# Expert rows fetched by indirect DMA from DRAM, slot numbers made on TensorE, and three more weight units loaded ahead

## The reference, cut to what matters

```python
def expert_choice_ffn(h, w_router, w_gate, w_up, w_down):
    cap = CAPACITY_FACTOR * S // N_EXPERTS                       # 64
    aff = jax.nn.softmax((h @ w_router).astype(jnp.float32), axis=-1)
    gates, idx = lax.top_k(aff.transpose(0, 2, 1), cap)          # each expert picks 64 tokens
    xe = h[bidx, idx]                                            # [expert, 64, 1024]
    hg = jnp.einsum('becd,edf->becf', xe, w_gate)
    hu = jnp.einsum('becd,edf->becf', xe, w_up)
    y = jnp.einsum('becf,efd->becd', jax.nn.silu(hg) * hu, w_down)
    y = y * gates[..., None].astype(y.dtype)
    return jnp.zeros_like(h).at[bidx, idx].add(y)                # scatter back
```

## Time and profile before

| | us |
|---|---|
| median of three runs | 2327.1 |
| the profiled execution, its own time | 2332.71 |
| its span, first to last instruction | 2330.9 |
| `experts`, first gather to the end | 1841.9 to 2330.9 |

### The profile page before, as it was taken

How to read it: one execution, slowest core, us unless ns; L and a number is a source line. 1 busy time by engine, 2 the same in 40 slices (tenths; PEclk the granted TensorE clock), 3 DMA queues, 4 the chain that set the end, 5 groups by cost and what they waited for, 6 DMA issues and landing times. The chain is left out here.

```text
span 2330.9 us, 31729 instructions
## 1 busy us (share of the span) xinstructions
PE 2087.4 (90%) x12841; PEld 1035.2 (44%) x12841; DVE 953.8 (41%) x1775; ACT 440.9 (19%) x877; POOL 238.9 (10%) x191
## 2 busy tenths in 40 slices
PE   6989898898998998989798977887789699999997
PEld 3453445643463343564343533455434444444442
DVE  1049668541026778752333542394321511111112
ACT  1011352121002144121312331321110200000000
POOL 0030410000020130000004530500000000000000
PEclk9999999999998999999899988998899799999999
DMA  4125110212214401121102101120055399999997
GB/s 158 68 107 198 46 39 26 75 46 69 80 48 172 163 10 39 35 101 36 48 18 73 37 28 48 62 77 34 11 163 207 128 403 419 421 420 420 420 420 290
DMA packets 63470, 330.03 MB, mean 142 GB/s; under 512 B 7280, under 2 KB 9840, under 8 KB 34928
## 3 DMA queue, kind: packets, MB, share of 16 engines
q1 hardware_dynamic: 63344, 328.27, 36.9%
HBM read 321.16 MB, written 6.29 MB: 140 GB/s over the span
## 5 line engine op out<-in xcount | busy, mean ns | idle before, releaser
L424 PE MATMUL ps<-store,side_ring 128*128 128x512 f32 x824 | 406.9, 623 | 15.8 <-DMA side_ring<-in_w_attn 7.1
L424 PEld LDWEIGHTS ps<-store,side_ring 128*128 128x128 f32 x824 | 146.0, 194 | 190.2 <-issue 168.3
L2565 PE MATMUL ps<-expert_ring,xe 128*64 128x512 f32 x1024 | 223.3, 593 | 4.0 <-DMA expert_ring<-in_w_expert 2.3
L337 PE MATMUL ps<-store,side_ring 128*128 128x512 f32 x384 | 169.9, 606 | 1.9 <-DVE store L303 1.9
L424 PE MATMUL ps<-store 128*128 128x512 f32 x256 | 122.1, 634 | 24.9 <-DMA store<-in_w_merge 24.4
L2565 PEld LDWEIGHTS ps<-expert_ring,xe 128*64 128x64 f32 x1024 | 73.0, 137 | 150.9 <-issue 148.7
L337 PEld LDWEIGHTS ps<-store,side_ring 128*128 128x128 f32 x384 | 74.5, 195 | 96.1 <-issue 93.5
L2593 PE MATMUL ps<-expert_ring,store 128*64 128x512 f32 x512 | 111.6, 594 | 1.4 <-DVE store L2650 1.4
L1645 PE MATMUL ps<-store,raw 128*128 128x512 f32 x256 | 110.7, 593 | 1.9 <-DVE store L303 1.9
L2622 ACT ACTIVATE store<-ps 128x1024 f32<-128x1024 f32 x16 | 16.4, 1025 | 417.8 <-PE ps L2565 417.8
L424 PEld LDWEIGHTS ps<-store 128*128 128x128 f32 x256 | 51.6, 204 | 93.1 <-issue 66.6
(11 more groups left out here) (430 smaller groups left out, 3051.4 us busy)
## 6 DMA issues: line engine op xcount, KB each, us to landing
expert_ring<-in_w_expert SPq DMA_DIRECT2D x192, 1024.0 KB, 17.1
mixed<-in_w_ada SPq DMA_DIRECT2D x24, 1024.0 KB, 4.8
side_ring<-in_w_attn SPq DMA_DIRECT2D x32, 512.0 KB, 3.9
side_ring<-in_w_rwkv SPq DMA_DIRECT2D x20, 512.0 KB, 4.4
raw<-in_ple_gate SPq DMA_DIRECT2D x16, 512.0 KB, 3.8
store<-in_w_merge SPq DMA_DIRECT2D x16, 512.0 KB, 4.1
side_ring<-in_w_conv SPq DMA_DIRECT2D x12, 512.0 KB, 3.3
gates_before<-gated SPq DMA_DIRECT2D x16, 256.0 KB, 2.0
```

The lines of the kernel that those rows point to most:

```text
L337: last = nc.tensor.matmul(ps[:, u, :], ring[:, u, k, :], src[:, k, :], start=(k == 0), stop=(k == kt - 1))
L424: ins = self.nc.tensor.matmul(self.ps[:, self.banks[j % banks], :], self.ring[:, j % self.slots, k, :], self.src[:, k, :], start=(k == 0), ...
L2565: last = nc.tensor.matmul(ps[w, 2 * ep + half, :], xe[:, ep, k, :], ring[:, unit % SLOTS, k2, S * half:S * half + S], start=(k == 0), stop ...
```

## The change

- **Rows.** SP writes `tokens` to DRAM as `token_rows` (four DMAs of 512 KB) once `h_copied` is complete. For pairs 1 to 7 POOL (GpSimd) fetches the 128 rows of a pair with one indirect DMA into a half of `rows` (the first two tiles of `tokens`). PE's gather becomes `turn_rows`: four transposes of the fetched rows after each eight transposes. The first pair's gather stays as it was.
- **Numbers.** `number` multiplies `chosen` of each later pair with a column of token numbers: 7 x 4 matmuls with one moving column, on PE between the first expert's products of pair 0 and `turn_back`. DVE casts the seven columns to integers.
- **Three units used once.** Units 0 to 2 of pair 0 go into places of their own, `once` (two in `back`, one new tile), issued when x is complete. The ring's first 12 units are then units 3 to 14, and SP's loop goes by turns of the ring.
- The loop over pairs has two pairs in its body, so that each unit's ring place is a constant. `route` takes its scratch from `chosen` instead of `back`.

The core of the diff:

```diff
@@ first_experts
-                sp.dma_start(ring[:, i], w_expert[0, i]).then_inc(landed[i], 16)
+                sp.dma_start(ring[:, i], w_expert[ONCE + i]).then_inc(landed[i], 16)
+            sp.wait_ge(added[0], added[1] + KT)
+            for i in range(ONCE):
+                sp.dma_start(once[i], w_expert[i]).then_inc(once_landed[i], 16)
@@ experts, sync
+                sp.wait_ge(h_copied, KT)
+                for t in range(TT):
+                    sp.dma_start(rows_out[t * P:(t + 1) * P, :], tokens[:, t, :]).then_inc(s["rows_out"], 16)
+                turns, rest = divmod(PAIRS * UNITS - ONCE, SLOTS)
+                with sp.Fori(1, turns) as turn:
+                    for i in range(SLOTS):
+                        sp.wait_ge(used[i], turn)
+                        sp.dma_start(ring[:, i], w_expert[turn * SLOTS + (ONCE + i)]).then_inc(landed[i], 16)
...
@@ experts, tensor
+                def number():
+                    for i in range(1, PAIRS):
+                        for t in range(TT):
+                            last = nc.tensor.matmul(ps[:, 3, i:i + 1], chosen[:, t, 2 * i:2 * i + 2, :].rearrange("p e c -> p (e c)"),
+                                                    M.c("token_number")[:, t:t + 1], start=(t == 0), stop=(t == TT - 1))
+                    last.then_inc(s["numbered"], 1)
+                def turn_rows(tiles, buf):
+                    for k in tiles:
+                        last = nc.tensor.transpose(ps[:, k // 4, (k % 4) * P:(k % 4 + 1) * P], rows[:, buf, k * P:(k + 1) * P],
+                                                   M.c("ident"))
+                        if k % 4 == 3:
+                            last.then_inc(s["gathered"], 1)
...
                             if first:
+                                number()
                                 turn_back()
...
                         if not final:
-                            gather(range(4 * ep, 4 * ep + 4), lambda t: chosen[:, t, bass.ds(r * 2 + 2, 2), :].rearrange("p e c -> p (e c)"))
+                            if ep == 0:
+                                pe.wait_ge(s["rows_landed"], r + 1)
+                            turn_rows(range(4 * ep, 4 * ep + 4), (1 + half_body) % 2)
@@ experts, gpsimd
+                pool.wait_ge(s["numbers_ready"], 1)
+                pool.wait_ge(s["rows_out"], 16 * TT)
+                pool.wait_ge(s["gathered"], 2)
+                for i in range(1, PAIRS):
+                    if i >= 3:
+                        pool.wait_ge(s["gathered"], 2 * (i - 1))
+                    nc.gpsimd.indirect_dma_start(rows[:, (i - 1) % 2, :], None, rows_out,
+                                                 bass.IndirectOffsetOnAxis(ap=numbers[:, i:i + 1], axis=0)).then_inc(row[i - 1], 16)
+                    pool.wait_ge(row[i - 1], 16)
+                    pool.sem_inc(s["rows_landed"], 1)
@@ experts, vector
+                dve.wait_ge(s["numbered"], 1)
+                nc.vector.tensor_copy(numbers[:, 1:PAIRS], ps[:, 3, 1:PAIRS]).then_inc(s["numbers_ready"], 1)
```

More of the change, by code:

```diff
@@ L2460, with slot_of, turn_of, first_experts @@
 PAIRS, UNITS, SLOTS = 8, 24, 12
-TURNS = UNITS // SLOTS
-def first_experts(nc, ring, w_expert, landed, busy, merge_taken, merge_done):
+BODY, ONCE = 2, 3
+TURNS = BODY * UNITS // SLOTS
+def slot_of(half, i):
+    return (UNITS * (1 + half) + i - ONCE) % SLOTS
+def turn_of(b, half, i):
+    return b * TURNS + (UNITS * (1 + half) + i - ONCE) // SLOTS
+def first_experts(nc, ring, once, w_expert, landed, once_landed, busy, merge_taken, merge_done, added):
     with phase(nc) as (block, s):
@@ L2485, in experts @@
         sb = lambda name, shape: buffer(nc, stack, name, shape)
-        xe = sb("xe", [P, 2, KT, 64])
+        xe, rows = sb("xe", [P, 2, KT, 64]), tokens[:, 0:2, :]
+        numbers = stack.enter_context(nc.sbuf_tensor(f"numbers_{nc.next_id()}", [P, PAIRS], U32))
+        w_expert = w_expert.rearrange("r u p k n -> (r u) p k n")
+        row = [stack.enter_context(nc.semaphore(f"row_landed_{i}")) for i in range(1, PAIRS)]
         flat = lambda first, tiles: room[:, first:first + tiles, :].rearrange("p k n -> p (k n)")
@@ L2499, in _ @@
             def _(sp):
[L2500 to L2507, removed]
+                sp.wait_ge(h_copied, KT)
[6 more added lines that the diff above has]
+                        sp.dma_start(ring[:, i], w_expert[turn * SLOTS + (ONCE + i)]).then_inc(landed[i], 16)
+                for i in range(rest):
+                    sp.wait_ge(used[i], turns)
+                    sp.dma_start(ring[:, i], w_expert[turns * SLOTS + ONCE + i]).then_inc(landed[i], 16)
+                sp.wait_ge(s["rows_landed"], PAIRS - 1)
                 for m in range(KT):
@@ L2602, in _ @@
                 pe.wait_ge(s["all_chosen"], TT)
[L2603 to L2606, removed]
+                pair(-1, 1, first=True)
+                with pe.Fori(0, PAIRS // BODY - 1) as b:
+                    for half_body in range(BODY):
+                        pair(b, half_body)
+                pair(PAIRS // BODY - 1, 0, final=True)
                 pe.wait_ge(s["out_ready"], PAIRS)
@@ L2641, in _, with pair @@
                 both = ps[:, 0:2, :].rearrange("p b (k e c) -> p e (b k) c", e=2, c=64)
-                def pair(r, first=False, final=False):
+                def pair(b, half_body, first=False, final=False):
+                    r = b * BODY + (1 + half_body)
                     if not first:
@@ L2674, in _ @@
                     nc.vector.tensor_copy(back[:, i, :], ps[:, 4 + i % 4, :]).then_inc(s["back_copied"], 1)
[L2675 to L2678, removed]
+                pair(-1, 1, first=True)
+                with dve.Fori(0, PAIRS // BODY - 1) as b:
+                    for half_body in range(BODY):
+                        pair(b, half_body)
+                pair(PAIRS // BODY - 1, 0, final=True)
                 for m in range(KT):
@@ L2724, in second_block @@
             ready = norm(nc, M, x, lambda k: gains[:, 1, k:k + 1], h, shift=lambda k: mcol(3, k), source=added)
[L2725 to L2728, removed]
+            h_copied, first_chosen = route(nc, M, a["w_router2"], h, ready, tokens, aff, chosen, slot,
+                                         chosen[:, :, :, :].rearrange("p t e c -> p t (e c)")[:, :, 0:S])
+            first_experts(nc, ring, once, a["w_expert2"].rearrange("r u p k n -> (r u) p k n"), landed, once_landed, busy, taken,
+                          multiplied, added)
+            experts(nc, M, a["w_expert2"], token_rows, tokens, chosen, aff, slot, extra[:, :], h, back, lambda j: mcol(5, j), x, out, ring, landed,
+                    once, once_landed, h_copied, first_chosen)
 def program(nc, a, out):
```

47 lines of the change are left out of this document (32 added, 15 removed).

## The result

The changed kernel takes 2339.43 us (median of 5 runs, 2337.67 to 2341.62), the kernel before 2327.1 us beside it (5 runs, 2325.43 to 2329.39): the ratio is 1.0054, with a 95% interval from 1.0038 to 1.007. It is slower, by 12.3 us between the medians; the forecast was 2336.4, 9.3 slower.

What follows compares the result with a forecast made beforehand. The weight stream on saturated DMA engines was taken as the bound, PE close behind. Terms -7.5 + 8.8 + 3.5 + 1.0 + 6.3 - 1.8 = +10.3 us, less 1.0 slack, gave +9.3: 2336.4 us, range 2332 to 2342.

Steps and rivals of the forecast that it cites:

- the hole: Empty weight stream behind pair 0's first expert, as number delays the second: +6.3 us left after two fetches fall into it.
- The bound: In the pairs, the saturated weight stream (DMA share 1.01, 420 GB/s) sets the end, slower than PE by 1.5 us a pair.
- Three units, -7.5: Three units of pair 0 move in idle time before the stream, which carries 177 units instead of 180: -7.5 us.
- first issue, +3.5: Start of the stream: the first ring place comes free one quarter later, at 1857.9, costing +3.5 us.
- Fetches, +8.8: Seven indirect fetches of 0.524 MB share the saturated engines with the weights at 1.25 us each: +8.8 us.
- the old stall: Stream's standstill of about 1.8 us from 1896 to 1900, during pair 0's transposes and gather, nearly closes: -1.8 us.
- Slack, -1.0: At the end, last bytes land about 1 us before use, so that much stream delay is absorbed: -1.0 us.
- Cheap numbers and free fetches: Rival: number takes only 1.7 us and fetches in the stream cost nothing; middle about 2329 us, no change, chance 0.22.
- TensorE the bound: Rival: PE limits the pairs, so seven shorter middles come back: -21 us, 2306 us, chance 0.08.
- A fetch on few engines: Rival: a fetch's rows go through one engine, 20 us each, holding the stream up to 140 us: up to 2467, chance 0.08.
- The clock in the pairs: Rival: PE's waits of some 1.5 us drop its clock to 1.2 GHz: +105 us, 2432 us, chance 0.04.

Runs made afterwards that it cites:

- e7: Changed kernel without numbers, row copies and fetches, rows gathered by products, keeping the three units used once: ratio 1.0006 to the kernel before.
- e3: Changed kernel with no units in places used once (ONCE = 0): ratio 1.0052 to the kernel before.
- e6: Changed kernel with each of the seven fetches issued a second time after the first landed: ratio 1.0092 to the kernel before.
- e2: Changed kernel without the seven indirect fetches and their wait: ratio 1.0033 to the kernel before.
- e5: Changed kernel with the number products streaming 64 repeated columns instead of one: ratio 1.005 to the kernel before.
- e1: Changed kernel without the 28 number matmuls; two small ones write other row numbers, same fetch traffic: ratio 1.0028 to the kernel before.
- e4: Changed kernel with number moved from before turn_back to behind the second expert's products: ratio 1.0072 to the kernel before.
- e8: Kernel before with turn_back moved to pair 1, units 4, 5, 12 used once, only pairs 1 and 2 fetched: 2323.1 us, ratio 0.9985.
- e9: e8 without its two fetches, their numbers and the row copy; all pairs gathered by products: ratio 1.0002 to the kernel before.
- e10: Kernel before with only turn_back moved from pair 0 to pair 1, ahead of its scatter: ratio 1.0008 to the kernel before.

## Why the prediction was right

The direction, the mechanism (the stream is the bound, PE's shorter middle buys nothing, PE waits for units) and the place of the hole came out as forecast. Size: the runs are 12.3 us slower and PE's last wait for a unit ends 12.4 us later, where 9.3 were forecast. The last landing came 13.7 us later relative to the first product, where 10.3 were forecast; 1.3 of that is a gap ahead of the last two units (3.8 us from one landing to the next instead of 2.5), behind PE's last wait; what made it is open. The terms that were off all erred the same way, so no luck is in the number: it was 3 us low, inside its range.

- *The bound.* Right: the earlier trace rows already held it, share 1.01 at 420 GB/s, and it is the same after. That PE had waited only 2.3 us was indeed no sign of spare transfer time.
- *Three units, -7.5, and first issue, +3.5.* The packets of e7's stream take 447.8 us instead of before's 454.6, -6.8, a little less than 7.5; the issue comes +3.46 later. Each term is about right, but the three units also leave the stream empty earlier at the next wait, so that together they are worth 0.1 us in the changed kernel (e3) and 0.3 alone (e7). The prediction held this in its hole, as five places given back instead of eight.
- *Fetches, +8.8.* Right: 9.2 for seven by e6's packets. To the last wait 5.5 us (e2), as two of the seven first fetches lie in the hole, and 8.8 us (e6). On this path POOL's transfers share the engines with SP's, as the Trainium skill (DMA: Bandwidth & Descriptors, section Issuing engines are not separate DMA queues) has it; e6's doubled fetches show it.
- *The hole, 6.3 + 1.0 - 1.8 = +5.5.* Near, with a part mis-sized. By the packets the engines stand idle 7.3 us longer (6.7 after; -0.6 before, in which the old stall of 1.8 lies, as such sums run over), 6.0 without the 1.3 of that gap. The old stall did close: the DMA share is 0.99 and 1.07 in the two stretches of 2 us from 1896 to 1900. `number` was taken at 6.2 us, from the records of the gather at 0.112 us each; it took 8.1, and `turn_back` 6.6 instead of 5.6, because the granted clock fell to half. The nearest row had 128 columns. e5, with 64, returns both to 6.3 and 5.6 us, the figures of the forecast; its last landing is 10.8 us later than before's, where the sum has 10.3.
- *Slack, -1.0.* Wrong: it should have been 0. It was read at the last unit, which landed at 2309.8 and was wanted at 2310.9. But PE's last wait stands 16 units earlier, and there PE waited 1.26 us before the change already, so a delay of the stream up to that unit reaches the end whole. The 13.1 us of the stage are these 12.4 and 1.5 of half clock in the last down products, less 0.9 by which the end behind the last scatter was shorter. (The estimate of 1 us from landing to use was too long as well: at this wait PE starts 0.14 us after the landing, in both kernels.)
- *The rivals.* Cheap numbers and free fetches: no (8.1 us; 1.32 us a fetch). TensorE the bound: no, PE waits 26.4 us. A fetch on few engines: no, 8.4 us median to landing against the 20 that it would have needed at least. The clock in the pairs: no, at 21 waits of up to 1.4 us PEclk is 1.00 from 1910 to 2300. It fell at another place, with no wait: in `number`. But e6 comes near the rival: behind waits of 2.0 to 2.6 us the clock did fall in three pairs.

What stays open is the fall of the clock in the last down products. It shows in after, e1, e3, e4, e8, e9 and e10 (1.4 to 3.0 us) and not in before, e2, e5, e6 and e7. The waits ahead, 1.57 and 1.41 us, are alike in after, before and e2. Nor is it known why the scatter of pair 1 lost 1.7 us in e9 and nothing in e8 and e10. No run here separates the cause; that is why each stage stands beside the length of these products.

## What to carry to other kernels

Where a ring is fed by uses, taking units out of the stream helps only as far as the next use that the stream waits for: find which use that is, and bring *it* forward. Look for the last wait that the bound causes, and not for the last landing: the slack behind that wait took up nothing here. With two resources at nine tenths, a change that relieved one and loaded the other lost here; e8 won by relieving both a little. Small products put between large ones had to be priced with the clock that they left behind, not by the row of a wider product.

## What the runs showed of the hardware

- 56 records with one moving column and 128x128 weights took 8.1 us, and the granted clock fell from 1.00 to 0.50, that is from 2.4 to 1.2 GHz, within them, PE busy throughout. With 64 columns: 6.3 us, clock 1.00.
- An indirect fetch of 128 rows of 4 KB holds POOL for 0.94 to 1.15 us, and it lands after a median of 4.3 us in the hole (two fetches between 1860 and 1880) and 8.7 us in the full stream (four from 1910 to 2300). It takes 1.32 us of the stream (e6), against 1.25 for its bytes at 420 GB/s.
- With 21 waits of up to 1.4 us (after) the granted clock stayed at 1.00 in the pairs; behind waits of 2.04, 2.62 and 2.60 us (e6) 32 records took 8.8, 8.8 and 8.7 us instead of 7.1. Behind a wait of 1.73 us the same scatter took 9.59 us in e9 and 7.90 in e8.
